# Samples' part of a Mamba-2 scan: new states as one fp32r product per PSUM bank, output in four column groups

## The reference, cut to what matters

```
def ssd_scan(x, dt, A, B, C, h0):
    """Mamba-2 SSD, chunked form of h_t = exp(dt_t A) h_{t-1} + dt_t B_t x_t^T, y_t = C_t h_t."""
    ...
    y_diag = jnp.einsum('bcijgr,bcjgrp->bcigrp', W, x)
    decay_to_end = jnp.exp(cum[:, :, -1:] - cum)
    chunk_states = jnp.einsum('bcjgn,bcjgr,bcjgrp->bcgrpn', B, decay_to_end * dt, x)
    ...
    y_off = jnp.einsum('bcign,bcgrpn->bcigrp', C, h_starts) * jnp.exp(cum)[..., None]
```

## Time and profile before

| what | us |
|---|---|
| median of 3 runs (lowest, highest) | 1810.49 (1809.89, 1811.14) |
| the profiled execution | 1809.74 |
| its span | 1808.1 |
| PE busy | 1786.2 |
| DVE busy | 1088.7 |
| ACT busy | 770.4 |
| POOL busy | 449.7 |

### The profile page before, as it was taken

How to read it: one execution, slowest core, us unless ns; L and a number is a source line. 1 busy time by engine, 2 the same in 40 slices (tenths; PEclk the granted TensorE clock), 3 DMA queues, 4 the chain that set the end, 5 groups by cost and what they waited for, 6 DMA issues and landing times.

```text
span 1808.1 us, 33921 instructions
## 1 busy us (share of the span) xinstructions
PE 1786.2 (99%) x12701; PEld 1753.3 (97%) x12701; DVE 1088.7 (60%) x2004; ACT 770.4 (43%) x1139; POOL 449.7 (25%) x352
## 2 busy tenths in 40 slices
PE   8999999999999999999999999999999999999998
PEld 7999999999998889999889999999999999999998
DVE  5577888999788777865866433444334433344434
ACT  6443435555356565632443333433234332333342
POOL 1577776777651111222100000000000000000132
PEclk9999999999999999999999999999999999999999
DMA  8665554555555555564334544445444454445442
GB/s 251 175 188 155 143 158 140 152 151 144 157 151 163 158 168 166 161 212 149 117 117 149 166 151 140 140 153 163 149 140 140 157 165 144 140 143 159 156 143 88
DMA packets 287349, 278.36 MB, mean 154 GB/s; under 512 B 11638, under 2 KB 284766, under 8 KB 286384
## 3 DMA queue, kind: packets, MB, share of 16 engines
q1 hardware_dynamic: 249112, 247.87, 45.0%
q10 hardware_dynamic: 36496, 21.77, 4.1%
q0 software_dynamic: 1648, 7.43, 1.3%
HBM read 261.25 MB, written 17.22 MB: 154 GB/s over the span
## 4 chain that ended last, share of the span: by engine, by line
PE 93%; ACT 3%; DVE 3%; issue 0%; DMA 0%; ACTq 0%; SPq 0%; DVEq 0%
PE ps L1799 28%; PE ps L1801 28%; PE ps L1800 28%; PE ps L1858 1%; PE ps L2082 1%; PE ps L1860 1%; PE ps L1859 1%; PE ps L2091 1%; PE ps L2032 1%; PE ps L2126 1%; PE ps L2128 1%; PE ps L2127 1%; PE ps L2055 0%; DMA xn<-in_x_prompt 0%; DVE wlo L1204 0%
## 5 line engine op out<-in xcount | busy, mean ns | idle before, releaser
L1799 PE MATMUL ps<-ahi,whi 128*128 128x320 f32 x2304 | 719.7, 312 | 4.1 <-DVE wlo L1204 4.1
L1801 PE MATMUL ps<-ahi,wlo 128*128 128x320 f32 x2304 | 713.5, 310 | 0.0
L1800 PE MATMUL ps<-alo,whi 128*128 128x320 f32 x2304 | 713.5, 310 | 0.0
L677 ACT ACTIVATE whi<-raw 128x1024 fp32r<-128x1024 f32 (+1 forms) x467 | 479.6, 1048 | 451.7 <-PE ps L1801 385.6
L1204 DVE TENSOR_TENSOR wlo<-raw,whi 128x1024 fp32r<-128x1024 f32 x347 | 423.9, 1244 | 247.7 <-ACT whi L677 245.0
L1799 PEld LDWEIGHTS ps<-ahi,whi 128*128 128x128 f32 x2304 | 433.5, 188 | 6.1 <-issue 4.5
L1800 PEld LDWEIGHTS ps<-alo,whi 128*128 128x128 f32 x2304 | 433.4, 188 | 0.5
L1801 PEld LDWEIGHTS ps<-ahi,wlo 128*128 128x128 f32 x2304 | 433.2, 188 | 0.0
L1799 PE MATMUL ps<-hhi,whi 128*128 128x320 f32 x1016 | 314.7, 310 | 0.0
L1801 PE MATMUL ps<-hhi,wlo 128*128 128x320 f32 x1016 | 314.4, 309 | 0.0
L1800 PE MATMUL ps<-hlo,whi 128*128 128x320 f32 x1016 | 314.4, 309 | 0.0
(11 more groups left out here) (316 smaller groups left out, 1636.5 us busy)
## 6 DMA issues: line engine op xcount, KB each, us to landing
raw<-in_w_in SPq DMA_DIRECT2D x144, 512.0 KB, 3.7
raw<-in_w_up SPq DMA_DIRECT2D x128, 512.0 KB, 4.3
raw<-in_w_down SPq DMA_DIRECT2D x128, 512.0 KB, 4.4
raw<-in_w_out SPq DMA_DIRECT2D x64, 512.0 KB, 3.6
h<-in_state_ssm ACTq DMA_DIRECT2D x16, 512.0 KB, 4.7
out<-hout ACTq DMA_DIRECT2D x16, 512.0 KB, 3.3
x_transposed<-xt ACTq DMA_DIRECT2D x1, 2560.0 KB, 9.8
xr<-x_transposed POOLq DMA_DIRECT2D x1, 2560.0 KB, 9.9
```

The costliest lines, as they stand in the source:

```text
L677: act.activation(whi[:, kq, :, 0:width], raw[:, kq, :, 0:width], ACT.Copy).then_inc(hi_done, 1)
L1799: pe.matmul(out, wh, hi[:, kk, :], start=(kk == 0), stop=False)
L1800: pe.matmul(out, wh, lo[:, kk, :], start=False, stop=False)
L1801: last = pe.matmul(out, wl, hi[:, kk, :], start=False, stop=(kk == NT - 1))
```

## The change: what it does

`bm` is replaced by `bq`, fp32r, 128 rows deep, and `xdd`'s sample rows by two tiles `xq[h]`, fp32r, one for each bank. Four stripes of 32 rows are stacked in both, so that one product of 128 rows sums high times high, and the cross terms of high and low parts, over a bank's tokens. Rows 64 to 127 of `xq[h]` are x's high part (ACT, two copies), rows 32 to 63 its own tokens' high part again (ACT, two copies), rows 0 to 31 the rest (DVE, two subtractions). In `bq` rows 64 to 127 are B's high part, masked (DVE), rows 32 to 63 the rest, masked (DVE, two halves), rows 0 to 31 the high part again (ACT, two copies of 32x512, in j = 0, after `hts`). PE waits for `xq_ready` and `bq_ready` ahead of L2082's place. L2091 becomes 32 matmuls with four quarters of 32 columns. `yoff` and `ysum` change places on DVE, since `yoff` now shares its memory with `s0s`.

The diff, without the semaphores' declarations:

```diff
-        bm = place("bm", [P, NB, P], at=sc + 1024)
+        bthi = place("bthi", [P, P], F32R, at=sc)
+        btlo = place("btlo", [P, P], at=sc + P)
+        bq = place("bq", [P, NB, P], F32R, at=sc + 1024)
...
-        s0s = place("s0s", [P, P], at=sc + 3968)
+        s0s = place("s0s", [P, P], at=sc + 4096)
...
+        xq = [place("xq0", [P, P], F32R, at=sc + 3968), place("xq1", [P, P], F32R, at=sm + 4352 + GROUPS * TOK)]
...
             def stage_b(i):
                 if not (isinstance(i, int) and i == 0):
                     act.wait_ge(cb_done, i)
+                    act.wait_ge(bq_ready, 2 * i)
...
                         act.activation(btok[:], ps[:, 4, 0:384].rearrange("p (c n) -> p c n", c=3), ACT.Copy
                                        ).then_inc(btok_ready, 1)
+                        act.wait_ge(btok_ready, i + 1)
+                        act.wait_ge(cb_done, i + 1)
+                        act.activation(bthi[64:P, :], btok[64:P, 2, :], ACT.Copy).then_inc(bthi_done, 1)
...
                     act.activation(h0t[:, 4:8, :], ps[:, 7, :].rearrange("p (b n) -> p b n", b=4), ACT.Copy
                                    ).then_inc(h0t_ready, 1)
+                    act.wait_ge(xd_ready, T + 1)
+                    if not first:
+                        act.wait_ge(st_done, T)
+                    for h in range(2):
+                        act.activation(xq[h][64:P, :], xdd[64:P, 2, :], ACT.Copy).then_inc(xhi_done, 1)
+                    for h in range(2):
+                        last = act.activation(xq[h][32:64, :], xdd[64 + 32 * h:96 + 32 * h, 2, :], ACT.Copy)
+                    last.then_inc(xq_ready, 1)
...
                     act.activation(hts[:], ps[:, 4, 384:512], ACT.Copy).then_inc(hts_ready, 1)
+                    if j == 0:
+                        act.wait_ge(bq_rows, i + 1)
+                        for h in range(2):
+                            last = act.activation(bq[0:32, 4 * h:4 * h + 4, :],
+                                                  bq[64 + 32 * h:96 + 32 * h, 4 * h:4 * h + 4, :].bitcast(F32), ACT.Copy)
+                        last.then_inc(bq_ready, 1)
                     decay(T, 1)
...
-                        dve.wait_ge(btok_ready, i + 1)
+                        dve.wait_ge(bthi_done, i + 1)
                         if not first:
                             dve.wait_ge(st_done, 4 * i)
-                        dve.tensor_tensor(bm[:], btok[:, 2, :].unsqueeze(1).to_broadcast([P, NB, P]),
-                                          blk[:].unsqueeze(2).to_broadcast([P, NB, P]), ALU.mult
-                                          ).then_inc(bm_ready, 1)
+                        dve.tensor_tensor(bq[64:P, :, :], bthi[64:P, :].bitcast(F32).unsqueeze(1).to_broadcast([64, NB, P]),
+                                          blk[64:P, :].unsqueeze(2).to_broadcast([64, NB, P]), ALU.mult
+                                          ).then_inc(bq_rows, 1)
+                        dve.tensor_tensor(btlo[64:P, :], btok[64:P, 2, :], bthi[64:P, :].bitcast(F32), ALU.subtract
+                                          ).then_inc(btlo_done, 1)
+                        dve.wait_ge(btlo_done, i + 1)
+                        for h in range(2):
+                            own = slice(64 + 32 * h, 96 + 32 * h)
+                            last = dve.tensor_tensor(bq[32:64, 4 * h:4 * h + 4, :],
+                                                     btlo[own, :].unsqueeze(1).to_broadcast([32, 4, P]),
+                                                     blk[own, 4 * h:4 * h + 4].unsqueeze(2).to_broadcast([32, 4, P]),
+                                                     ALU.mult)
+                        last.then_inc(bq_ready, 1)
+                    dve.wait_ge(xhi_done, 2 * T + 2)
+                    for h in range(2):
+                        own = slice(64 + 32 * h, 96 + 32 * h)
+                        last = dve.tensor_tensor(xq[h][0:32, :], xdd[own, 2, :], xq[h][own, :].bitcast(F32), ALU.subtract)
+                    last.then_inc(xq_ready, 1)
...
-                pe.wait_ge(bm_ready, i + 1)
+                pe.wait_ge(xq_ready, 2 * T + 2)
+                pe.wait_ge(bq_ready, 2 * i + 2)
                 for h in range(2):
-                    own_rows = slice(64 + 32 * h, 96 + 32 * h)
-                    pe.matmul(ps[:, 6 + h, :], xdd[own_rows, 2, :], bm[own_rows, 4 * h:4 * h + 4, :],
-                              start=True, stop=True)
+                    pe.matmul(ps[:, 6 + h, :], xq[h][:], bq[:, 4 * h:4 * h + 4, :], start=True, stop=True)
...
                 for b in range(NB):
-                    for e in range(2):
-                        pe.matmul(ps[e * HD:(e + 1) * HD, 5, 448 + DS * b:456 + DS * b],
-                                  h0t[:, b, e * HD:(e + 1) * HD],
+                    for e in range(4):
+                        quarter = slice(e * P // 4, (e + 1) * P // 4)
+                        pe.matmul(ps[quarter, 5, 448 + DS * b:456 + DS * b], h0t[:, b, quarter],
                                   xb[:, NT + GROUPS + i, SEQ + DS * b:SEQ + DS * (b + 1)], start=True, stop=True)
```

More of the change, by code:

```diff
@@ L267, in build @@
             sem("var_root"), sem("cn_done"), sem("silu_done"))
-        bt_ready, bt_trans, btok_ready, bm_ready, cb_done = (
-            sem("bt_ready"), sem("bt_trans"), sem("btok_ready"), sem("bm_ready"), sem("cb_done"))
+        bt_ready, bt_trans, btok_ready, bq_ready, cb_done = (
+            sem("bt_ready"), sem("bt_trans"), sem("btok_ready"), sem("bq_ready"), sem("cb_done"))
+        bthi_done, btlo_done, bq_rows = sem("bthi_done"), sem("btlo_done"), sem("bq_rows")
+        xhi_done, xq_ready = sem("xhi_done"), sem("xq_ready")
         xst_ready, xtile_trans, xd_ready, seg_done, exp_done, mixw_done = (
@@ L1579, in wc @@
                     dve.wait_ge(y_done, T + 1)
-                    v1 = st.inc(dve.tensor_tensor(yoff[:], ps[:, 5, TOK:512], ecb[:], ALU.mult))
-                    v2 = st.inc(dve.scalar_tensor_tensor(
+                    v1 = st.inc(dve.scalar_tensor_tensor(
                         out=ysum[:], in0=xb[:, T, :], scalar=par[:, T, R_DSKIP:R_DSKIP + 1],
                         in1=ps[:, 5, 0:TOK], op0=ALU.mult, op1=ALU.add))
+                    dve.wait_ge(pst_done, T + 1)
+                    v2 = st.inc(dve.tensor_tensor(yoff[:], ps[:, 5, TOK:512], ecb[:], ALU.mult))
                     dve.wait_ge(dve_step, v2)
```

## The result

The changed kernel takes 1823.8 us, the median of six runs (1821.74 to 1826.0); the kernel before, run beside it, takes 1810.61 (1809.75 to 1811.14, six runs). The ratio is 1.0075, with a 95% interval of 1.0064 to 1.0085 (the ratios given here are the record's own estimates, not quotients of the medians): slower by 13.2 us, clearly more than the 0.2% that can be told. One run of the kernel before, beside a later experiment, took 2493.86 us at a mean granted clock of 0.65 and is left out of the medians. The forecast was 1811.9, with a range up to 1817.0. Both missed.

The account below looks back on a forecast made before the run. The prediction took PE as the bound, busy 1786.2 of 1808.1 us. Its terms, -6.0 + 2.2 + 0.35 + 2.8 + 2.0 = +1.35 us, gave 1811.1 for the profiled execution and 1811.9 for the median, range 1805.0 to 1817.0.

Parts of the forecast that it names:

- (a): L2082 on PE: as one fp32r product per bank, 0.46 us against 1.06, so L2085 starts 0.62 us earlier.
- two records of about 0.23 apart: Sign in the changed profile: the new product on PE shows as two records about 0.23 us apart.
- (b): L2091 on PE: four column groups run side by side, 64 records for 32, the block taking 0.51 us.
- a record costs its 0.030 whatever its width: Rival on L2091: four groups don't run side by side, the block takes 1.90 us, kernel 1826.2; chance 0.08.
- (c): Ordinary steps: L2055 waits for DVE's mask and starts 0.67 us earlier; nine steps, -6.0 us.
- (f): Steps with j = 0, delayed by ACT's bq copies and DVE: T = 4 +0.35, T = 8 and 12 +1.4 each, T = 0 +2.0.
- (d): ACT between h0t and the weight split: four xdd copies at 0.18 us each, 0.72 per step, hidden in ordinary steps.
- the upper bound: Upper end for ACT's four copies: 0.28 us each, 1.11 in all.
- ACT's copies cost a full record: Rival on ACT: copies at 0.28 us each because waits between them break the overlap, kernel 1815.4; chance 0.20.
- (e): j = 1 of i = 1, 2, 3: ACT has no gap, so the copies' 0.72 us passes to the end, +2.2 in all.
- The PE wait: Sign in j = 0: PE waits about 1.5 us in front of the product, ended by ACT's bq copy.

Follow-up runs that it names:

- the whole-tile copies: The changed kernel with xq's two high copies over all 128 rows instead of rows 64 to 127: 1823.59 us, ratio 1.0074.
- the filled kernel: The changed kernel with PE's wait in j = 0 filled by bf16 products that nothing reads: 1820.71 us, ratio 1.0057.
- rows that do not move: The changed kernel with ACT's 32-row copies and bq's low-row copies read from the same rows that they write: 1818.4 us, ratio 1.0042.

## Why the prediction was wrong, and where it was right

**(a) The product: right in what it brings, short in its size.** In T = 6 L2123 starts 0.79 behind L2111, where L2085 started 1.40 behind L2072: 0.61 earlier for 0.62 forecast. But the sign "two records of about 0.23 apart" did not come: they start 0.31 to 0.32 apart in fifteen steps and 0.56 in T = 0, which is at half clock. In T = 8, where hts is long done, the product takes 0.55 (669.66 to 670.21) for 0.46. An ordinary step hides this, since L2123 waits for hts there and the product starts 0.17 behind L2111 instead of 0.25. xq was in time in all steps with j = 2 and 3; in j = 1 PE waited some 0.4 for it, ahead of a longer wait for hts.

**(b) The four column groups: right.** First to last record of the block 0.55 us, in every step in which it ran at full clock, and 0.65 to the start of L2055 with the groups alone; forecast were 0.51 for the block and 0.10 to 0.17 behind it. Before, 0.90 and 0.95. The rival in which a record costs its 0.030 whatever its width is out. On the Trainium skill's floor of about 25 ns from start to start ("TensorE: Matmul & The Clock Gate", section "Wait — 56ns, not 53.3ns?"), the sum would have been near 1822, an estimate from the page, and close to the result by accident: 64 records within 0.55 us are under 9 ns each, so for four column groups side by side the measurement decides, and it is against that floor.

**(c) The ordinary step: right.** -0.67 in five of the nine steps, with the mask as what PE waits for. T = 6 and 10 gave -0.41, because the shift of DVE's reciprocal was 1.7 us and not 1.28, more than the 1.34 that covers it: the copies and DVE's two subtractions both took longer than costed. T = 14 gave +1.13, through the clock. T = 1 is the ninth, and is counted with T = 0 in (f).

**(d) The price of ACT's copies: the step that failed first.** It went by hts, 0.18 to the next. That row is of a tile on all 128 rows behind another such tile. The new copies start at rows 64, 96 and 32, and in none of these traces did such an instruction overlap with a neighbour whose first row differs. Measured they are 1.32 us for the four, 0.60 more than forecast and 0.2 above the upper bound, which counted four records and not the loss of h0t's own overlap. The rival "ACT's copies cost a full record" named the price, though not the reason (it took the waits between the copies for it, which the whole-tile copies rule out ahead of the first one), and its 1815.4 was still low.

**(e) j = 1: +1.10 for +0.72,** twice (T = 5, 9). In T = 5 the copies put the table load 1.79 behind h0t instead of 0.61.

**(f) j = 0: too low throughout, for the same reason.** For T = 8: ACT's four copies +0.60, bq +0.40, and 0.16 on PE behind the product: +2.58 for +1.4. T = 4 +0.92 for +0.35; T = 0 with T = 1 +3.1 for +1.3, where DVE's new work was also costed short: from btlo to the split behind xq's two subtractions it is 2.34 us (558.23 to 560.57) for 1.8. The PE wait was foretold as about 1.5 us. That fits T = 4, where 1.75 was measured. For T = 8 and 12 the prediction's own terms (product at 665.98, PE free for it at about 663.4) give 2.5, and 3.4 was measured. That slip mattered: the length of this wait was never put to use.

**What was missing: the granted clock, a term put at nothing without a reason.** No part of the prediction asks what PE's clock does after a wait of 2 to 4 us in a stretch that had none. In the profiled run this is about +0.4 in T = 12, 1.0 in T = 13 and 1.5 in T = 14, read against T = 8, 9 and 10, at most 3 of the scan's 10.8. On the medians the filled kernel gives 3.1 us back, net of its own loss.

So the scan's 10.8 in the profiled run is 1.3 as forecast, 2.9 from the clock, and the remaining 6.6 from the true price of ACT's copies and of the DVE work beside them, in steps with j = 0 and 1, and in T = 6, 10 and 14. How it divides between the two engines is argued from the rows of single steps. That ACT's copies carry most of it is shown by themselves: alone, and with the waits filled, they cost 5.8, where the forecast's price gives 3.6; with rows that do not move some 2 us come back by the rows, and 5.4 in the medians. That the clock falls because PE waits is shown twice by filling. Not settled is in which steps it falls: T = 8 and T = 12 have a wait of 3.42 us each in the profiled run, and behind T = 8 the clock stayed at 1.00; so it did behind the mask waits of 1.42 us in T = 5 and 9, and not behind that in T = 13. This varies from run to run, which fits the spread of 4.3 us among six runs, against 1.4 for the kernel before.

## What to carry to other kernels

Price a small copy by a row of the same kind in the same place: if its first row differs from its neighbours', count the whole record, and the overlap that the instruction ahead of it loses. When PE is 98% busy at full clock, a new wait on it costs its length and may cost as much again behind it: 5.8 and 7.1 us in the kernel with ACT's copies alone. Work that nothing reads, in the place of the wait, can be cheaper than waiting. And of a change with two halves, cost each alone: here the column groups gain 2.9 us, and the product that buys PE's time with ACT's loses 21.5 without them and 16.4 on top of them.

## What the runs showed of the hardware that was not expected

**Overlap depends on the first row.** On ACT, start to start against the length of the first: a 64-row copy behind another on the same rows 0.22 of 0.29; a 32-row copy from rows 64 and 96 to row 32 0.32 of 0.31; a 32x512 copy from rows 64 and 96 to row 0 0.64 of 0.63, and 0.52 of 0.61 when both start at row 0; behind h0t 0.61 with row 64 and 0.47 with row 0 (0.59 long). The new copies of the changed kernel in one view, with shortest, median and longest ns:

```profile
L1037 ACT ACTIVATE xq<-xdd x32: 290/300/311, 557.5 to 764.5; 64x128 fp32r<-64x128 f32 x32
L1039 ACT ACTIVATE xq<-xdd x32: 307/308/310, 558.1 to 765.1; 32x128 fp32r<-32x128 f32 x32
```

A copy of 32 rows is no shorter than one of 64. DVE shows the same as ACT: its two subtractions of 0.28 span 0.58 (T = 6, above), so they do not overlap.

**The clock fell behind waits of about a microsecond.** In the kernel with the copies alone PE waited 0.94 us for hts in T = 8, until 669.58, and the clock was at the lower of its two levels (1.2 and 2.4 GHz) from 671.0 to 677.8, so that T = 9 ran at 0.83 of full speed over 17.5 us. In T = 5 it waited 1.04 us for the mask, until 629.88, and the lower level lasted from 630.0 to 633.5. Waits of 1.42 us in T = 5 and 9 of the changed kernel had no such effect, so a wait of this length does not always do it.

**The narrow block feels the clock.** The 64 records span 0.55 us in fourteen steps, and 0.84 in T = 0 and T = 12, where it falls into a stretch at the lower level (558.9 to 565.7 and 726.1 to 729.6).

**The DMA issue of pst on ACT's queue lasts 0.42 us in the median and now and then 0.9 to 2.1.** The issues of hout and of the old states, on the same queue, stayed between 0.38 and 0.43 in the kernel before and the changed one. Why is open; it costs time only where ACT has no slack left.
